# Hybrid attention and mLSTM block: projections and output product as Strassen passes, low parts of weights on GpSimd

## The reference

```python
proj = rms_norm(x) @ w_in
oa = rms_norm(diff_attention(q, k, v)) * 0.8          # 8 heads
ob = sigmoid(ml_o) * rms_norm(mlstm(...))             # 8 heads
h = x + (g0 * (oa @ w_proj_a) + g1 * (ob @ w_proj_b)) @ w_out
h = h + relu(rms_norm(h) @ w_ff1)**2 @ w_ff2
return rms_norm(h)
```

## Time and profile before

| what | value |
|---|---|
| three runs, median | 1883.43 us (1883.35 to 1883.46) |
| the profiled execution | 1883.48 us |
| its span, first to last instruction | 1881.3 us |
| mean granted TensorE clock | 0.998 of full |
| busy: TensorE, VectorE, ScalarE, GpSimd | 1871.9, 1183.4, 949.5, 329.8 us |
| moved by DMA | 293 MB, 156 GB/s in the mean |

### The profile page before, as it was taken

One profiled execution on the slowest core, in us unless ns is written; L12 is line 12 of the kernel. 1 busy time (PEld: TensorE's weight loads), 2 busy tenths in 40 slices (PEclk: granted clock), 3 DMA queues, 4 the chain that ended last, 5 costly groups with the idle time before them and its releaser, 6 DMA issues.

```text
span 1881.3 us, 26892 instructions
## 1 busy us (share of the span) xinstructions
PE 1871.9 (100%) x9832; PEld 1606.0 (85%) x9832; DVE 1183.4 (63%) x1621; ACT 949.5 (50%) x1541; POOL 329.8 (18%) x182
## 2 busy tenths in 40 slices
PE   9999999999999999999999999999999999999998
PEld 6989898989898989888888888888888888888887
DVE  7675858585767676544311122787868778688774
ACT  5455655556565656445333232236676585333343
POOL 1202020211111111132224444420000000021002
PEclk9999999999999999999999999999999999999999
DMA  6351515151514242432254444557668587464312
GB/s 222 100 171 56 192 57 195 51 199 51 181 64 158 84 159 89 162 120 77 73 185 146 151 135 173 182 182 268 233 236 286 192 284 255 168 227 153 151 74 90
DMA packets 103283, 293.19 MB, mean 156 GB/s; under 512 B 10888, under 2 KB 27912, under 8 KB 92192
## 3 DMA queue, kind: packets, MB, share of 16 engines
q1 hardware_dynamic: 100896, 283.69, 43.5%
q10 hardware_dynamic: 2304, 8.39, 1.1%
HBM read 204.94 MB, written 87.10 MB: 155 GB/s over the span
## 4 chain that ended last, share of the span: by engine, by line
PE 99%; DVE 1%; POOL 0%; DVEq 0%; issue 0%; POOLq 0%
PE gp L755 14%; PE gp L753 14%; PE gp L754 14%; PE scores L1025 6%; PE scores L1027 6%; PE scores L1029 6%; PE gp L773 3%; PE gp L771 3%; PE gp L772 3%; PE gp L1025 2%; PE gp L1027 2%; PE gp L1029 2%; PE scores L871 2%; PE scores L870 2%; PE ob L918 2%; PE ob L919 2%
## 5 line engine op out<-in xcount | busy, mean ns | idle before, releaser
L753 PE MATMUL gp<-r1h,w_hi 128*128 128x512 f32 x880 | 346.7, 394 | 0.0
L755 PE MATMUL gp<-r1h,w_lo 128*128 128x512 f32 x880 | 343.7, 391 | 0.0
L754 PE MATMUL gp<-r1l,w_hi 128*128 128x512 f32 x880 | 342.8, 390 | 0.0
L1025 PE MATMUL scores<-xh,qh 128*128 128x512 f32 x512 | 199.7, 390 | 0.1
L1029 PE MATMUL scores<-xh,ql 128*128 128x512 f32 x512 | 199.2, 389 | 0.0
L1027 PE MATMUL scores<-xl,qh 128*128 128x512 f32 x512 | 199.2, 389 | 0.0
L755 PEld LDWEIGHTS gp<-r1h,w_lo 128*128 128x128 f32 x880 | 165.2, 188 | 35.1
L753 PEld LDWEIGHTS gp<-r1h,w_hi 128*128 128x128 f32 x880 | 165.4, 188 | 32.9
L754 PEld LDWEIGHTS gp<-r1l,w_hi 128*128 128x128 f32 x880 | 165.4, 188 | 32.6
L2077 POOL TENSOR_TENSOR w_lo<-w_raw,w_hi 128x1024 fp32r<-128x1024 f32 x25 | 60.6, 2423 | 490.6 <-ACT w_hi L1128 467.1
L773 PE MATMUL gp<-w_hi_pair,r1l 128*128 128x256 f32 x512 | 144.8, 283 | 0.0
(11 more groups left out here) (346 smaller groups left out, 4250.7 us busy)
## 6 DMA issues: line engine op xcount, KB each, us to landing
xraw<-xo_d SPq DMA_DIRECT2D x54, 1024.0 KB, 5.1
w_raw<-in_in_blocks SPq DMA_DIRECT2D x64, 512.0 KB, 3.7
proj_d<-ev SPq DMA_DIRECT2D x128, 256.0 KB, 2.4
rq<-in_ff_quarters SPq DMA_DIRECT2D x32, 1024.0 KB, 7.8
xo_d<-res SPq DMA_DIRECT2D x78, 256.0 KB, 3.4
xo_d<-ring SPq DMA_DIRECT2D x60, 256.0 KB, 3.5
gt<-proj_d SPq DMA_DIRECT2D x32, 256.0 KB, 3.7
xt<-in_x_halves SPq DMA_DIRECT2D x8, 512.0 KB, 7.1
```

The costliest lines, as they stand in the source:

```text
L753: pe.matmul(gp[half][:], wh[slot][:, k, :], mh[:, k, t], start=(k == 0), stop=False)
L754: pe.matmul(gp[half][:], wh[slot][:, k, :], ml[:, k, t], start=False, stop=False)
L755: mm = pe.matmul(gp[half][:], wl[slot][:, k, :], mh[:, k, t], start=False, stop=(k == KT - 1))
L1025: pe.matmul(bank, qh[s % 3][:, k, cols], xh[s % 3][:, k, :], start=first and k == 0, stop=False, skip_group_check=True)
```

## The change

The three products of the projections become groups of seven Strassen passes ahead of the feed-forward's eight groups, so that one loop runs over 11 groups, 77 passes. Their input differences are made from the heads' outputs in DRAM: for three of four column blocks by GpSimd within the last head's round (`turn_item`, four operations of 128x512 per block), for the last one by VectorE (`turn_late`). Results of a pass are copied by ScalarE (idx 0, 2, 3) or added by VectorE (idx 1, 5, 6); the gates are applied by GpSimd (`gated`, twelve operations of 128x512 per projection) and VectorE (`gated_bank`, idx 4), the branches are merged by VectorE (`merged`, sixteen operations). At the start of `w_out` (pass 14, `S_WO`) and of the feed-forward (pass 21, `S_F1`) VectorE forms sixteen sums and differences straight from the results, which go to DRAM for later passes. `scaled` applies the norm (16 operations of 128x512 with both inputs in SBUF), and GpSimd sums the squares (`square_sum`). The low part of the x quarter stays on VectorE. The low part of each weight quarter, in the feed-forward too, moves from VectorE to GpSimd (`q_lo_part`), but for the first three; the semaphore of all low parts is parted in one for weights and one for x. Weight blocks of the projections and their GpSimd splits go; DMAs of 1 MB quarters come in their place. The core of the diff:

```diff
+G_PA, G_PB, G_WO, G_F1 = range(4)
+G_F2 = G_F1 + GROUPS
+NG = G_F2 + GROUPS
+STAGES = NG * NP
...
 def stage_unit(s, u, between=None):
     g, idx = divmod(s, NP)
+    at = (s + 1) % 3
     if u == 0:
-        pe.wait_ge(p_lo, 2 * s + 2)
+        pe.wait_ge(q_low, s + 1)
+        pe.wait_ge(xq_low, s + 1)
     if idx in SET_A:
         bank = bank_a[u]
         if s:
             pe.wait_ge(ev_a, 4 * UN * g + UN * (SET_A[idx] - 1) + u + 1)
-        elif u == 0:
-            pe.wait_ge(s_ready, 2)
+        if s == S_F1 and u == 0:
+            pe.wait_ge(s_ready, 3)
     else:
         bank = bank_b[u]
         if s > 1:
             pe.wait_ge(ev_b, 3 * UN * g + UN * (SET_B[idx] - 1) + u + 1)
         elif u == 0:
+            pe.wait_ge(gp_free, 2 * N_PA)
+            pe.wait_ge(obt, 2 * NH)
+        if s == S_WO + 5 and u == 0:
+            pe.wait_ge(s_ready, 1)
+        if s == S_F1 + 5 and u == 0:
             pe.wait_ge(d_ready, 2)
...
 def q_hi_part(s):
     g, idx = divmod(s, NP)
     if s == 0:
-        act.wait_ge(gemm_done, 2 * N_WO)
-    elif s < 3:
-        act.wait_ge(gemm_done, 2 * N_FF)
-    else:
+        act.wait_ge(ta_st, 64 * (UN - 1))
+        act.wait_ge(tb_st, 64 * (UN - 1))
+    elif s > 2:
         act.wait_ge(mm_done, UN * (s - 2))
     if idx in (0, 1, 4):
         q = {0: 0, 1: 1, 4: 3}[idx]
         act.wait_ge(rq_in[q], 16 * (g + 1))
     else:
         act.wait_ge(q_sum, sums_at(g, {5: 1, 2: 2, 3: 3, 6: 4}[idx]))
-    act.activation(qh[s % 3][:], quarter_of(s)[:], ACT.Copy).then_inc(p_hi, 1)
+    act.activation(qh[(s + 1) % 3][:], quarter_of(s)[:], ACT.Copy).then_inc(p_hi, 1)
+def x_hi_part(s):
+    to = xh[(s + 1) % 3]
+    if s in FROM_RES:
+        second = s in (S_WO + 1, S_F1 + 1)
+        act.wait_ge(m_done if s < S_F1 else xs_done, UN * (1 + second))
+        act.activation(to[:], res[:, UN * second:UN * second + UN, 0:HALF], ACT.Copy).then_inc(p_hi, 1)
+        return
+    if s in FROM_SUMS:
+        act.wait_ge(bt_done, BT[s >= S_F1] + 2 * UN)
     else:
+        act.wait_ge(xq_in[s % 2], x_loads(s))
+    act.activation(to[:], x_from(s)[:], ACT.Copy).then_inc(p_hi, 1)
...
+def wide_sums(beta, u, b12, to):
+    dve.tensor_tensor(ta[:, u, :], res[:, UN + u, HALF:], b12, ALU.subtract).then_inc(bt_done, 1)
+    dve.wait_ge(bt_done, BT[beta] + 2 * u + 1)
+    dve.tensor_tensor(to, ta[:, u, :], res[:, u, 0:HALF], ALU.add).then_inc(bt_done, 1)
+def narrow_sum(beta, u, b12):
+    dve.tensor_tensor(b12, b12, res[:, u, 0:HALF], ALU.subtract).then_inc(bt_done, 1)
+def last_sum(beta, u, t2, to):
+    if u == 0:
+        dve.wait_ge(bt_done, BT[beta] + 2 * UN)
+        if beta:
+            dve.wait_ge(h1_st[C12], 16)
+            dve.wait_ge(sq_ready, 4 * UN)
+    dve.tensor_tensor(to, res[:, UN + u, 0:HALF], t2, ALU.subtract).then_inc(bt_done, 1)
...
+def q_lo_first(s):
+    at = (s + 1) % 3
     dve.wait_ge(p_hi, 2 * s + 1)
-    dve.tensor_tensor(ql[s % 3][:], quarter_of(s)[:], qh[s % 3][:].bitcast(F32), ALU.subtract).then_inc(p_lo, 1)
+    dve.tensor_tensor(ql[at][:], quarter_of(s)[:], qh[at][:].bitcast(F32), ALU.subtract).then_inc(q_low, 1)
...
+def gated_bank(s, u):
+    g = s // NP
+    n = gate_tile(g, C21, u)
+    dve.wait_ge(mm_done, UN * s + u + 1)
+    dve.wait_ge(g_sig, n + 1)
+    dve.tensor_tensor(res[:, UN + u, 0:HALF] if g == G_PA else gts[n % GT], bank_a[u], gts[n % GT],
+                      ALU.mult).then_inc(ev_a, 1)
+def merged(c, u):
+    k, half = tile_of(c, u)
+    to = res[:, k, half * HALF:(half + 1) * HALF]
+    if c == C21:
+        dve.wait_ge(ev_a, a_out(G_PB, 4, u))
+        src = gts[gate_tile(G_PB, C21, u) % GT]
+    else:
+        dve.wait_ge(g_used, pool_gated(G_PB, c, u))
+        src = (ta if c == C12 else tb)[:, u, :]
+    dve.tensor_tensor(to, to, src, ALU.add).then_inc(m_done, 1)
+def residual(s, u):
+    idx = s % NP
+    i, c = {0: (0, C11), 2: (1, C12), 3: (2, C22), 4: (3, C21)}[idx]
+    k, half = tile_of(c, u)
+    src = (tx, ta, tb, ta)[i]
+    if u == 0:
+        dve.wait_ge(x_in[IN_REST + i], X_LOADED[IN_REST + i] + 16)
+        if idx == 0:
+            dve.wait_ge(bt_done, BT[0] + 4 * UN)
+        if idx in (2, 3):
+            dve.wait_ge((st_t1, st_b22)[idx - 2], 16)
+    dve.wait_ge(mm_done, UN * s + u + 1)
+    dve.tensor_tensor(res[:, k, half * HALF:(half + 1) * HALF], bank_a[u], src[:, u, :], ALU.add).then_inc(ev_a, 1)
...
+elif s == S_WO:
+    for u in range(UN):
+        merged(C12, u)
+        dve.wait_ge(m_done, 3 * UN + u + 1)
+        wide_sums(0, u, res[:, u, HALF:], xraw[1][:, u, :])
+    for u in range(UN):
+        narrow_sum(0, u, res[:, u, HALF:])
+    x_lo_part(s + 2)
+    for u in range(UN):
+        last_sum(0, u, xraw[1][:, u, :], tb[:, u, :])
+elif s == S_F1:
+    for u in range(UN):
+        scaled(C22, u)
+    for u in range(UN):
+        scaled(C12, u)
+    for u in range(UN):
+        dve.wait_ge(xs_done, 3 * UN + u + 1)
+        wide_sums(1, u, tb[:, u, :], xraw[0][:, u, :])
+    for u in range(UN):
+        narrow_sum(1, u, tb[:, u, :])
+    x_lo_part(s + 2)
+    for u in range(UN):
+        last_sum(1, u, xraw[0][:, u, :], res[:, u, HALF:])
+elif s in (S_WO + 1, S_F1 + 1):
+    weight_sum(g, 3)
+    for u in range(UN):
+        add_bank(s, u)
+    x_lo_part(s + 2)
+elif g == G_WO:
+    if idx == 4:
+        x_lo_part(s + 2)
+        root(0)
+        for u in range(UN):
+            scaled(C11, u)
+    elif idx == 5:
+        weight_sum(g + 1, 1)
+        x_lo_part(s + 2)
+    elif idx == 6:
+        for u in range(UN):
+            scaled(C21, u)
+        weight_sum(g + 1, 2)
+        x_lo_part(s + 2)
+        token_var(1)
+    else:
+        if idx == 3:
+            weight_sum(g, 4)
+        x_lo_part(s + 2)
 else:
-    if idx == 1:
+    if idx == 1 and g:
         weight_sum(g, 3)
-    if 1 <= g <= GROUPS and idx == 1:
-        hidden_turned(g - 1, 3)
-    if idx == 3 and g:
+    if G_F1 < g <= G_F2 and idx == 1:
+        hidden_turned(g - G_F1 - 1, 3)
+    if idx == 3:
         weight_sum(g, 4)
-    if g < 2 * GROUPS - 1 and idx in (5, 6):
+    if g < NG - 1 and idx in (5, 6):
         weight_sum(g + 1, idx - 4)
     if s + 2 < STAGES:
-        q_lo_part(s + 2)
         x_lo_part(s + 2)
-    if 1 <= g <= GROUPS and idx == 0:
+    if G_F1 < g <= G_F2 and idx == 0:
         for u in range(3):
-            hidden_turned(g - 1, u)
-if g > GROUPS or idx in (1, 5, 6):
+            hidden_turned(g - G_F1 - 1, u)
+    if g == G_PB and idx in (2, 6):
+        for u in range(UN):
+            merged(C11 if idx == 2 else C22, u)
+if g == G_WO and idx in SET_A:
+    for u in range(UN):
+        residual(s, u)
+    if idx == 3:
+        token_var(0)
+elif g in (G_PA, G_PB) and idx == 4:
+    for u in range(UN):
+        gated_bank(s, u)
+    for u in range(UN if g else 0):
+        merged(C21, u)
+elif (g > G_F2 or idx in (1, 5, 6)) and s not in (S_WO + 1, S_F1 + 1):
     for u in range(UN):
...
         add_bank(s, u)
+        if s == S_F1 - 1 and u == 1:
+            root(1)
...
+def q_lo_part(s):
+    at = (s + 1) % 3
+    if s == 3:
+        pool.wait_ge(q_low, 3)
+    pool.wait_ge(p_hi, 2 * s + 1)
+    pool.tensor_tensor(ql[at][:], quarter_of(s)[:], qh[at][:].bitcast(F32), ALU.subtract).then_inc(q_low, 1)
+def gated(g, c, u):
+    n = gate_tile(g, c, u)
+    k, half = tile_of(c, u)
+    t = res[:, k, half * HALF:(half + 1) * HALF] if g == G_PA else (ta if c == C12 else tb)[:, u, :]
+    pool.wait_ge(g_sig, n + 1)
+    pool.wait_ge(ev_b, b_out(g, {C11: 1, C22: 5, C12: 6}[c], u))
+    pool.tensor_tensor(t, t, gts[n % GT], ALU.mult).then_inc(g_used, 1)
+def square_sum(n):
+    half = n // (2 * UN)
+    a = sqacc[:, half * HALF:(half + 1) * HALF]
+    pool.wait_ge(sq_ready, n + 1)
+    pool.wait_ge(ss_done, half + 1)
+    wait(pool, sq_used, square_added(n) - 1 if n not in (1, 2 * UN + 1) else 0)
+    pool.tensor_tensor(a, a, uts[n], ALU.add).then_inc(sq_used, 1)
...
+for s in range(STAGES):
+    g, idx = divmod(s, NP)
+    if s and s + 2 < STAGES:
+        q_lo_part(s + 2)
+    if g < G_WO and idx in (1, 5, 6):
+        for u in range(UN):
+            gated(g, {1: C11, 5: C22, 6: C12}[idx], u)
+    if S_WO <= s <= S_F1:
+        for n in {3: range(1, 4), 5: range(4, 8), 6: range(9, 12), 7: range(12, 16)}.get(s - S_WO, ()):
+            square_sum(n)
+    if H1_FROM <= s < H1_FROM + KT:
+        h1_scale(s - H1_FROM)
+    if g == NG - 1 and idx in (1, 4, 5, 6):
+        for u in range(UN):
+            n = UN * (1, 4, 5, 6).index(idx) + u
+            if n < 2 * KT - 1:
+                square_add(n)
```

More of the change, by code:

```diff
@@ L83 @@
 X_LOADED = (16, 16, 16, 32, 64, 16, 16, 16)
+IN_LATE, IN_REST, IN_ITEM = 0, 2, 6
 SLOTS = 16
@@ new lines, in turned_stores, with late_load @@
+            def turned_stores(buf, done, base, second, u):
+                for j, (op, at) in enumerate(((O_T1, 0), (O_T3, 1), (O_T2, 3), (O_T4, 2))):
+                    sp.wait_ge(done, base + j + 1)
```

(47 more changed lines are left out.)

820 lines of the change are left out of this document (388 added, 432 removed).

## The result

The changed kernel takes 1947.1 us (median of 4 runs, 1944.5 to 1947.5) against 1883.45 for the kernel before: a ratio of 1.0335, 95% interval 1.0317 to 1.0353. It is 64 us slower; the forecast was 26 us slower, and the range ended at 1938.

What follows compares the result with a forecast made beforehand. TensorE was taken to bound the kernel, busy the whole span. Fewer matmuls (-32.7 us) and new waits (19.7, 3, 3, 9, 5, 5, 13, 1) summed to +26 on 1883.43: 1909 us, own range 1890 to 1930, whole range 1866 to 1938.

Steps and rivals of the forecast that it cites:

- Gain: Projections: products fall from 1152 to 1008 matmuls, 144 x 0.2267 us, so -32.7 us, whole unless waits appear.
- GpSimd's low part and the collision: A weight low part takes 4.6 us on GpSimd (VectorE 2.28) and blocks VectorE operations with two SBUF inputs throughout.
- Rival A: Low parts fit into VectorE's idle gaps; stalls of 10 us in all, 1861 us; chance 0.12.
- B: Rival: only the feed-forward waits, the projections hold; 1873 us; chance 0.14.
- four ends of first-layer groups: Feed-forward, first layer to second: three chain links lengthen by 7.1 us, less slack; TensorE waits 19.7 us (10 to 35).
- group with the residual: Feed-forward: port time of 84 us exceeds 76.2, half hides under PSUM adds; +3 us (0 to 6).
- into the output product (pass 16): VectorE's work ahead of the residual add that frees pass 16's bank takes 28 to 34 us against 21.8; +9 (7 to 12).
- pass 19 to 20: Output product: root, reciprocal, scaling and x low part stand ahead of the add; +5 us (0 to 9).
- into the feed-forward (pass 23): VectorE operations, sums of squares, a low part and an x part total 34 us against 21.8; +13 (8 to 20).
- start: Late in the gates SP queues some 10 MB ahead of gate stores that ScalarE's copies wait for; +1 us (0 to 7).
- C: Rival: everything piles up, boundaries give 54 us instead of 36, feed-forward 5 more; 1933 us; chance 0.13.
- D: Rival: half-speed TensorE clock after boundary stalls, three times 12 us lost; 1921 us; chance 0.12.

Runs made afterwards that it cites:

- e7: e1 plus 26 GpSimd subtractions of 128x2048 in otherwise unused SBUF, awaited by nobody, from the tenth feed-forward pass to the residual's group; 1936.6 us, 1.0286.
- e4: Changed kernel, low parts of weights still on GpSimd; from the fifth feed-forward pass ScalarE makes the x high part before the weight's; 1912.3 us, 1.0163.
- e1: Changed kernel with every low part of a weight operand back on VectorE, the rest of the change kept; 1890.6 us, 1.0046 of the kernel before.
- e5: e1 with ScalarE's bank copies first at the feed-forward's entry, waiting for the third kind of differences only; 1887.6 us, 1.0025 of the kernel before.
- e6: e1 with SyncE's loads and stores at the end of the gates spread out; 1881.55 us, 0.9995 of the kernel before.
- e2: Changed kernel with weight low parts back on VectorE from the first feed-forward pass on, the three square products' left on GpSimd; 1903.0 us, 1.0112.
- e3: Kernel before, with only the low parts of feed-forward weights (passes 3 to 55) moved to GpSimd; projections untouched; 1924.8 us, 1.0228.
- e9: e8 with four more orders: residual add earlier at two output-product passes, column sums half a pass later, third feed-forward pass's copies earlier; 1875.1 us, 0.9959.
- e8: e1 with both the spread SyncE list of e6 and the ScalarE entry order of e5; 1879.9 us, 0.9986 of the kernel before.
- e10: e9's orders with weight low parts left on GpSimd and the x high part first from the sixth feed-forward pass; 1902.1 us, 1.0102 of the kernel before.

## Why the prediction was wrong in size, and right in sign

**Gain, right.** -32.7 us (144 x 0.2267 is 32.6): 144 matmuls fewer, and the 0.2267 between two starts is unchanged where TensorE does not wait.

**GpSimd's low part and the collision, right.** 4.6 us was the estimate; alone it took 4.61, its means of 4.7 to 5.2 hold some standing still of its own. VectorE's x low part was expected at 3 us or more and has 4.36 in the mean. e7 shows the exclusion by itself, e4 that the order of issue decides who pays: by the Trainium skill (SBUF — State Buffer, "Who interferes with whom") issue order picks the winner, and the pair of e4 agrees in both directions, 2.29 us undisturbed when VectorE came first and 5.10 instead of 0.68 when it came second. Rival A (they fit) fell with the waits at the group ends, and B (the projections hold) with the waits between 1130 and 1300 us in the table.

**The waits, term by term** (start to start less one matmul):

| step of the prediction | forecast us | measured us |
|---|---|---|
| four ends of first-layer groups | 19.7 | 17.1 |
| group with the residual | 3 | 6.5 |
| second projection, pass 5 to 6 | 3 | 2.1 |
| into the output product (pass 16) | 9 | 8.9 |
| pass 16 to 17 | 5 | 6.5 |
| pass 19 to 20 (TensorE stops at the column sums in pass 19) | 5 | 6.7 |
| into the feed-forward (pass 23) | 13 | 14.7 |
| start | 1 | 5.7 |
| last group, end of its banks | not named | 4.8 |
| first projection (0.9), behind the column sums (1.0), into pass 21 (1.6) | not named | 3.5 |
| sum | 58.7 | 76.6 |

The chains behind the boundaries gave sizes close to the measured ones. In one term that is partly luck. **Into the feed-forward** I had added up VectorE's work only; in the trace TensorE waits there for ScalarE's copies, which stand behind a weight high part that waits for VectorE's last sum:

```profile
1294.06 1.91 ACT L1451 ACTIVATE qh<-rq 128x2048 fp32r<-128x2048 f32 x1 [7.37 <-DVE rq L2020]
1295.87 2.04 ACT L1511 ACTIVATE res<-scores 128x512 f32<-128x512 f32 x4
```

The wait is still 12.2 us without any low part of the loop on GpSimd (e1), and e5, which turns this order on ScalarE, brings it to 5.0, with another of 3.6 at the next pass. In the group with the residual the eight adds on VectorE took 3.97 us each and not 1.2, so less hid than the half that I assumed. Two terms were missed. **The start** I priced at 1 of a range of 0 to 7, reasoning that TensorE did not wait there before. But SyncE's list puts 6 MB ahead of a store for which a copy waits, and the store lands behind them:

```profile
971.24 0.60 ACT L1244 ACTIVATE ev<-gp 128x512 f32<-128x512 f32 x1 [13.78 <-DMA proj_d<-ev]
```

e6 shows that it is this, and 9.0 us with the clock behind it. **The last group** I left out: TensorE waits there too, for the adds out of the banks (L2057), 4.8 us at 1877. As I read it, this is the same chain of three links; that it comes with GpSimd's low parts is shown by e2, where it is gone, and e3, where it is there.

**The clock: the step that failed.** I gave "each boundary stall might be followed by such a stretch" a chance of 0.12 and a price of 12 us, and put nothing of it into the sum. The trace now shows a stretch at 1.2 GHz behind each of the ten waits of 4.2 us or more from start to start, 3.4 to 13.7 us long, also behind the four in the feed-forward, which I had not counted. Slow matmuls grew from 2 to 22 us, so **+20** where the sum had 0. "HAM oscillation" of the Trainium skill (TensorE: Matmul & The Clock Gate) says that an array left waiting for data comes back at the lower clock; the trace agrees, though most waits here are for a bank to be read and not for data, and it was right to weigh it, wrong to leave it at one in eight. I had argued that the waits of the trace before were too short to tell, which is a reason for keeping both ends and not for zero. No experiment changed the clock alone; what it cost is read from the spacing of the matmuls, and it goes wherever a wait goes (e1: 10 us of slow matmuls instead of 22, and e9: 9).

Together: 26 + 19 (waits, 78 more than before where the sum had 58.7) + 20 (clock) = 65, where the spans differ by 64.2 and the medians by 63.6. Either of the two alone would have ended inside the range, at 1928 or 1929. The range left their sum out since cases C (more waits) and D (the clock) stood as alternatives, while they are effects that add up: more waits bring more low clock.

**Where the gain went, by experiment.** Low parts on GpSimd: 44 us in the feed-forward (e2, e3 from the other side 43) and 12.5 in the square products. The new stream's own boundaries: about 40 (e1 has 33 us of waits and 8 of slow matmuls more than the kernel before), of which the start is 9 (e6) and orders another 6 (e8, e9). The gain of fewer matmuls: -32.7. 56.5 + 40 - 33 = 64. What stays of those 40 in e9 lies mostly beside VectorE's work between 1144 and 1265 us, which has 9 us of idle time in it. That this work is the cause is argued and not shown: whether a shorter reciprocal or fewer scalings there would give the rest was not tried.

## What to carry to other kernels

A busy share says nothing of a shared port: before moving an elementwise operation from VectorE to GpSimd, add both engines' SBUF instructions along each chain that frees a bank, at GpSimd's duration, and ask which of two colliding instructions is issued first; if it must move, put it behind the one on the chain (e4 gained 35 us by this, yet e10 still lost 27 to e9). Price each wait of TensorE by more than its length, since a stretch at half clock can follow, as it did behind the ten longest waits of the kernel after: 20 us on 79. And where a store has a waiter, count the megabytes that SyncE issues ahead of it.

## What the runs showed of the hardware that I had not expected

- Two low parts in a row on GpSimd took 11.63 us together, 5.8 each where one alone took 4.61, with a VectorE low part of 5.40 between them:

```profile
1384.18 11.63 POOL L2344 TENSOR_TENSOR ql<-rq,qh 128x2048 fp32r<-128x2048 f32 x2 [14.67 <-ACT qh L1451]
```

```profile
1385.94 5.40 DVE L1990 TENSOR_TENSOR xl<-xraw,xh 128x2048 fp32r<-128x2048 f32 x1 [1.18 <-ACT xh L1464]
```

- Work that nobody waits for can cost 46 us: the 26 idle GpSimd subtractions of e7 took 127 us of an engine that had nothing else to do in those passes.
- A single matmul gap of 3.4 us (the column sums in e1 and e8) was already followed by a stretch at the lower clock, 3.4 us long in e1 and 6.8 in e8. A gap of 2.9 us in the residual's group was followed by one in e3 (3.4 us long) and not in the kernel after, and a gap of 4.2 us at 1329 in e10 was followed by none. So the length of a wait alone did not tell here whether the clock would fall.
